# Between the mLSTM heads, the filling weight products are issued in halves with one group of small products between two halves

## The reference, cut to what matters

```python
hq, hf, hi, hgate, mq, mk, mv, mo, mig, mfg = split_cols(h @ w_in, SPLIT_SIZES)
hg_o = hgrn2_chunkwise(silu(hq), 1.0 - forget, hi, log(forget))
hg_o = rms_norm(hg_o, hg_norm) * silu(hgate)
mq, mk = split(silu(causal_depthwise_conv(concat([mq, mk]), conv_w, conv_b)), 2)
# mlstm, per head, D[t, s] = b_t - b_s + log_i_s for s <= t, m_t its running maximum
num = (q @ k.T * exp(D - m)) @ v
den = sum over s of (q @ k.T * exp(D - m))
h   = num / maximum(abs(den), exp(-m))
ml_o = rms_norm(h, ml_norm) * sigmoid(mo)
return concat([hg_o, ml_o]) @ w_out
```

## Time and profile before

| | us |
|---|---|
| three runs, median (lowest to highest) | 2395.99 (2393.27 to 2400.38) |
| the profiled execution | 2393.68 |
| its span between first and last instruction | 2392.3 |
| PE busy in it | 2329.0 (97%) |
| DVE, ACT, POOL busy | 829.9, 449.5, 1279.4 |

### The profile page before, as it was taken

The page is one execution under the profiler, slowest core; times in us unless marked ns, Lnnn a source line. Parts: engine busy times, 40 slices in busy tenths (PEclk is TensorE's granted clock), DMA queues, the critical chain, the costliest instruction groups (busy, mean ns, idle before and its releaser), DMA issues.

```text
span 2392.3 us, 26085 instructions
## 1 busy us (share of the span) xinstructions
PE 2329.0 (97%) x11060; PEld 1915.3 (80%) x11060; DVE 829.9 (35%) x872; ACT 449.5 (19%) x736; POOL 1279.4 (53%) x734
## 2 busy tenths in 40 slices
PE   7999999999999999999999999999999999999999
PEld 6888888887778888888888887877657788888887
DVE  2323104884343333005232105320578632333013
ACT  2111003323222111003111002011357121111011
POOL 4666665633255666665666665555100556666654
PEclk9999999999899999999999999999889999999999
DMA  4333332212023333332333332223000223333322
GB/s 157 97 97 97 97 97 80 80 45 62 27 87 99 97 97 97 97 97 72 97 97 97 97 97 89 79 90 98 19 1 1 71 88 97 97 97 98 105 85 83
DMA packets 55580, 201.06 MB, mean 84 GB/s; under 512 B 6408, under 2 KB 6536, under 8 KB 55336
## 3 DMA queue, kind: packets, MB, share of 16 engines
q1 hardware_dynamic: 53712, 193.62, 26.1%
q10 hardware_dynamic: 1752, 5.77, 0.6%
HBM read 197.27 MB, written 2.10 MB: 83 GB/s over the span
## 4 chain that ended last, share of the span: by engine, by line
PE 90%; DVE 6%; ACT 2%; issue 1%; DMA 1%; POOL 0%; ACTq 0%; DVEq 0%; POOLq 0%
PE psum L341 19%; PE psum L343 18%; PE psum L342 18%; PE psum L401 7%; PE psum L403 7%; PE psum L402 7%; PE psum L479 2%; PE psum L894 1%; PE psum L886 1%; PE psum L381 1%; ACT junk L1108 1%; DVE x L1590 1%; PE psum L923 1%; PE psum L546 1%; PE psum L439 1%
## 5 line engine op out<-in xcount | busy, mean ns | idle before, releaser
L323 POOL TENSOR_SCALAR w_hi<-w_raw 128x1024 fp32r<-128x1024 f32 (+1 forms) x365 | 388.3, 1064 | 1066.0 <-PE psum L343 657.0
L325 POOL TENSOR_TENSOR w_lo<-w_raw,w_hi 128x1024 fp32r<-128x1024 f32 (+1 forms) x365 | 891.7, 2443 | 30.5
L341 PE MATMUL psum<-u_hi,w_hi 128*128 128x512 f32 (+1 forms) x2072 | 794.8, 384 | 10.7 <-DVE work L1938 4.7
L342 PE MATMUL psum<-u_hi,w_lo 128*128 128x512 f32 (+1 forms) x2072 | 788.9, 381 | 0.0
L343 PE MATMUL psum<-u_lo,w_hi 128*128 128x512 f32 (+1 forms) x2072 | 788.7, 381 | 0.0
L341 PEld LDWEIGHTS psum<-u_hi,w_hi 128*128 128x128 f32 x2072 | 391.9, 189 | 90.3 <-issue 7.4
L343 PEld LDWEIGHTS psum<-u_lo,w_hi 128*128 128x128 f32 x2072 | 391.6, 189 | 74.4
L342 PEld LDWEIGHTS psum<-u_hi,w_lo 128*128 128x128 f32 x2072 | 391.9, 189 | 73.8 <-issue 0.7
L401 PE MATMUL psum<-w_hi,hidden_hi 128*128 128x512 f32 x800 | 311.8, 390 | 1.0 <-DVE work L1797 1.0
L402 PE MATMUL psum<-w_lo,hidden_hi 128*128 128x512 f32 x800 | 311.2, 389 | 0.0
L403 PE MATMUL psum<-w_hi,hidden_lo 128*128 128x512 f32 x768 | 298.8, 389 | 0.0
(11 more groups left out here) (263 smaller groups left out, 1679.9 us busy)
## 6 DMA issues: line engine op xcount, KB each, us to landing
w_raw<-in_ffn_in SPq DMA_DIRECT2D x176, 512.0 KB, 3.5
w_raw<-in_ffn_out SPq DMA_DIRECT2D x88, 512.0 KB, 3.5
w_raw<-in_proj_in SPq DMA_DIRECT2D x34, 512.0 KB, 3.5
w_raw<-in_mix_in SPq DMA_DIRECT2D x29, 512.0 KB, 3.5
w_raw<-in_embed SPq DMA_DIRECT2D x10, 512.0 KB, 3.5
w_raw<-in_mix_out SPq DMA_DIRECT2D x8, 512.0 KB, 3.4
w_raw<-in_branch SPq DMA_DIRECT2D x8, 512.0 KB, 3.5
w_raw<-in_proj_out SPq DMA_DIRECT2D x8, 512.0 KB, 3.6
```

Source lines behind the costliest of these rows:

```text
L323: pool.tensor_scalar(hi, raw, 1.0, 1.0, ALU.mult, ALU.mult).then_inc(k.w_split, 1)
L325: pool.tensor_tensor(lo, raw, hi.bitcast(F32), ALU.subtract).then_inc(k.w_split, 1)
L341: pe.matmul(out, hi[:, cols], xhi, start=first, stop=False)
L342: pe.matmul(out, lo[:, cols], xhi, start=False, stop=False)
```

## The change

On PE the fills 12, 13, 14, 15, 24 and 25 are cut into two parts of 12 matmuls by a new function, and the groups of small products are dealt between the parts; fill 26, which stood behind the last head sums, now stands ahead of them. Fills 26 and 27 stay whole. On ACT `take(25)` changes places with `squares(H+3)`. Nothing is computed otherwise than before.

```diff
+def pe_dense_part(k, name, i, bank, part):
+    pe = k.nc.tensor
+    n, hi, lo = k.pair(name, i)
+    if part == 0:
+        pe.wait_ge(k.w_split, 2 * n + 2)
+    for t in range(part * KD // 2, (part + 1) * KD // 2):
+        m = mm3(pe, k.ps[bank], hi, lo, slice(t * P, (t + 1) * P), tile(k.uhi, t), tile(k.ulo, t), t == 0, t == KD - 1)
+    if part:
+        m.then_inc(k.w_used, 1)
...
+    def fill_part(i, part):
+        if part == 0:
+            wait_filled(k, pe, FILL[FILL.index(i) - 2])
+        pe_dense_part(k, "mix_in", i, fill_bank(i), part)
...
     pe_turn(k, g.mv_in, 0, 4 * NT)
-    fill(12)
+    fill_part(12, 0)
     logits(0)
-    fill(13)
+    fill_part(12, 1)
+    fill_part(13, 0)
     values(0)
+    fill_part(13, 1)
     logits(1)
-    fill(14)
+    fill_part(14, 0)
+    pe_head_sums(k, HEADS)
+    fill_part(14, 1)
     values(1)
-    pe_head_sums(k, HEADS)
+    fill_part(15, 0)
     logits(2)
-    fill(15)
+    fill_part(15, 1)
+    pe_head_sums(k, HEADS + 1)
+    fill_part(24, 0)
     values(2)
-    pe_head_sums(k, HEADS + 1)
+    fill_part(24, 1)
     logits(3)
-    fill(24)
+    fill_part(25, 0)
+    pe_head_sums(k, HEADS + 2)
+    fill_part(25, 1)
     values(3)
-    pe_head_sums(k, HEADS + 2)
-    fill(25)
+    fill(26)
     pe_head_sums(k, HEADS + 3)
-    fill(26)
     fill(27)
...
+    take(25, ACT.Sigmoid)
     squares(H + 3, tile(g.ml_out, 3))
-    take(25, ACT.Sigmoid)
     take(26, ACT.Sigmoid)
```

## The result

The changed kernel took 2397.81 us (median of 12 runs, 2392.33 to 2405.11), the kernel before 2394.01 us beside it (12 runs). The ratio is 1.0020, 95% interval 1.0012 to 1.0028: some 4.8 us slower (the medians differ by 3.8). The forecast was 2391.5 us, in a range of 2385 to 2397, with 0.71 on no difference above 0.3%. The difference is indeed under 0.3%, but the time lies outside the range, and the sign is the other one than the sum's: 3.3 us less were forecast.

What follows compares the result with a forecast made beforehand. PE was taken to bound the kernel, busy but at clock 0.90 in the stretch; 9.6 - 0.7 - 2.0 - 2.4 - 1.2 = 3.3 us less gave 2390.4 by execution, 2392.7 by median; forecast 2391.5 us, range 2385 to 2397.

Steps and rivals of the forecast that it cites:

- three falls of the clock: Half-clock drops inside logits of heads 1 to 3, lasting into the fills behind; all taken as gone, 9.6 us less.
- idle ahead of values(0): PE waits while ACT's take(12), ahead of decay(0), waits for the whole of fill 12; 2.0 us, ends 0.3 and 3.0.
- idle ahead of the sums of head 2: PE waits for hd_sq, which ACT counts behind decay(3), two table loads, Silu and take(24); 2.4 us, ends 1.5 and 3.
- joints: Six more starts of large runs behind small products on PE, 0.11 us each; 0.7 us in all, ends 0 and 1.5.
- end of the stage: Last head sums have one fill behind them, not two, so PE idles longer before the fourth output tile; 1.2 us more.
- Rival 4: Clock falls behind the stall at values(0) and halves of 12 large matmuls do not restore it; 2417 us, chance 0.06.
- every return lies inside a run of large products: Reading of the trace before: the clock always came back during large matmuls, taken as agreeing that activity releases it.
- Rival 3: Mix counts, not run length: all three falls stay and stalls are paid; 6.3 us slower, about 2400, chance 0.05.
- rivals 2 and 4: Rival 4, and one where one fall stays, at the stall of 2.0 us plus values(0): 2392 to 2394, chance 0.18.
- POOL's split: POOL's next slot, begun at the end of fill 27, likely to lie under DVE's first gate; up to 0.7 us more.

Runs made afterwards that it cites:

- halves repaired: Changed kernel with decay(0) ahead of take(12) on ACT and both last head sums behind fill 25, two whole fills behind them; ratio 0.9969 to the kernel before.
- decay first: Changed kernel with decay(0) ahead of take(12) on ACT; ratio 0.9997 to the kernel before.
- sums early: Changed kernel with values(3) half a fill behind logits(3) and both last head sums behind fill 25; ratio 1.0006 to the kernel before.

## Why the prediction was wrong, point by point

| step (us, plus is longer) | predicted | measured |
|---|---|---|
| three falls of the clock | -9.6 | +3.4 |
| idle ahead of values(0) | +2.0 | +1.96 |
| idle ahead of the sums of head 2 | +2.4 | +0.62; 2.24 once the first wait was gone |
| joints | +0.7 | +0.7 (halves repaired against before, at full clock) |
| end of the stage | +1.2 | +2.1 (fill 27 to the fourth tile: 8.5 us before, 10.6 after) |

**The step that failed** is "I therefore take all three falls as gone". It made one row, the 5.19 us at 642.71 with its fill at full clock, into a length that is safe. Two things were wrong with that. The row was one execution: in another, the same run was followed by a fall. And length alone did not decide: the run of `values` is shorter, 4.3 us, but its second half, 2.15 us, is twenty recorded matmuls of one column each, and within 1.3 us behind it the clock fell in the changed kernel for four heads of four (599.0, 619.5, 640.0, 660.5). The other four falls came behind the idle time ahead of `values(0)` (592.2) and at the end of the logits of heads 1 to 3 (605.9, 626.4, 646.8). That the one-column products have a part in it the experiments show: take them out and six of eight low stretches go; put six large matmuls among them, and with the repairs none is left. That they suffice is not shown: with the columns whole and the halves kept, the clock fell within 1.5 us behind them for one head of four with decay first, for three with the sums early and for two with both repairs. Cutting in halves made of three long falls (6.8 us) eight short ones (3.4 us), each with a loss of 1.7 us: 13.6 against 10.2.

Rival 4 had the right direction but not the right size: the clock did fall behind the stall of `values(0)`, but each low stretch lasted 3.4 us only. Five ended inside a half of 12 large matmuls, one inside fill 26 and one 0.4 us behind a half; the first, from 592.2 to 595.6, ended inside `values(0)`, with no large product since 590.2. Its premise that 12 do not bring the clock back is refuted, and so is the reading that every return lies inside a run of large products. (Its 2417 also takes the gain off a second time; 30 us on top of the 2390.4 are 2420.) Rival 3, the falls stay and the costs are paid, 6.3 us slower, comes nearest to what happened, though its three falls did not stay but became eight shorter ones; I gave it 0.05 on the ground of the same row.

**The waits.** The wait ahead of `values(0)` was right to 0.04 us, with its cause: take at 587.47 and decay at 587.96 on ACT, the mask done at 592.05 on DVE, L629 at 592.12:

```profile
587.47 0.59 ACT L1241 COPY work<-psum 128x512 f32<-128x512 f32 x1 [7.22 <-PE psum L343]
587.96 1.79 ACT L1337 ACTIVATE work<-psum,misc 128x512 f32<-128x512 f32 x4
```

That of the sums of head 2 was right as a chain (L616 at 643.07, squares at 651.20 + 0.62, 8.75 us later, against 8.6), but PE came 1.9 us late itself, at half clock, so that little was left to wait for. What the sum had not priced, and only rivals 2 and 4 had, is a fall of the clock behind an idle PE. Taking away 1.96 us of idle brought 5.5 us. That idle by itself does it is not shown: of the eight waits of 1.2 to 2.3 us among the heads in all traces seven were followed by a fall within 2.5 us, but the same 1.96 us in the kernel with early sums was not, nor was any of the six of 1.3 to 3.3 us at the spreads or the fourth tile.

**The end.** The sum named POOL's split as a risk of 0.7 us on the gate. It fell on the diagonals instead: the four tiles took 5.49 us at 672.66, where they took 2.50 before (663.77 to 666.27), as the last two of them, 1.52 and 2.83 us instead of 0.69, lay beside POOL's L323 (673.80 to 674.86) and L325 (674.95 to 677.61). The multiply ahead of them took 0.18, as I had said, where it had taken 1.24. So the new idle time of PE is not the 1.8 us that I had put ahead of the fourth tile (0.83 there), but 1.63 us ahead of the last spread. That the one engine makes the other longer was not tested by itself, but it holds in other traces: the same 1.52 and 2.83 us with decay first, where POOL stands beside them, and 0.69 for all four with the sums early, where it does not. The Trainium skill (SBUF — State Buffer, Who interferes with whom) has a DVE instruction with two SBUF inputs contend with a GpSimd one that reads SBUF; the trace agrees, with the 3 us.

**Still open** is what exactly counts. The same group was followed by a fall in one kernel or execution and not in the next: `logits(0)` in one trace and not in ten, the columns for one to four heads of four. An obvious rival was not tested: that the moment at which a group begins decides too. Every edit here moves all groups behind it in time, and each kernel but two was traced once, so the runs can't separate what stands in a group from when it stands there.

## What to carry to other kernels

A stretch of small products is judged by what is in it as well as by its length, and from several executions: one fill at full clock behind it proves nothing. When work is cut finer to keep the clock up, try the large products inside the groups and not only between them (here six among the one-column products took the ratio from 0.9969 to 0.9949), and check for each group that moves which count it needs and what stands ahead of that on the other engine: here `take(12)` ahead of `decay(0)` cost 5.5 us and the late sums 3.4, where the halves without both gain 7.4. A clock loss and a wait need not be independent terms: most waits among the heads were followed by a fall.

## What the runs showed of the hardware that I had not expected

- The granted clock fell while PE was busy in every slice: behind 2.15 us of one-column float32 products and 0.6 to 1.3 us of large ones, in the changed kernel.
- In the stretch of the change the clock stayed low for 3.4 us at a time in the changed kernel, where it had stayed low for 6.8; it came back mostly inside 12 large matmuls, and once (595.6) inside small products.
- Executions of the same kernel differ by up to 13 us (2392.33 to 2405.11 of the changed kernel); the low clock over the whole program was 62 to 65 us in all four traces of these two kernels, though 20.5 to 27.3 us of it in the stretch of the change.
